# A one-core encoder-trunk step: x rows loaded for the first norm, weight chunks cut as half the features by 512 columns, and more expert rows summed on VectorE

## The chip, the cores and the metric

The kernel runs as one launch on one core of a Trainium2 chip. The metric is the device time of one execution in microseconds (us), as the median of several runs. The profile is one profiled execution of the same program.

## The reference

One layer is computed for 1024 prompt rows and 32 sample rows of 1024 features, all in float32. The sample rows are repeated four times to fill a ninth tile of 128 rows.

```python
h = rmsnorm(x, g_norm1); z = h @ w_in                 # 3096 columns: GLA q,k,v,g; low rank; FoX q,k,v; forget
o_gla, S_new = gla_recurrence(gq, gk, gv, log_a, S0)  # gated linear attention
o_fox = fox_attention(rmsnorm(fq), rmsnorm(fk), fv, cumsum(logf))
x = x + concat(o_gla_normed * silu(gg), o_fox) @ w_out
h2 = rmsnorm(x, g_norm2)
q = h2 @ w_peer_q                                     # 8 heads, two keys each of 128
s1, s2 = top16 of the products with 128 subkeys each; 16 best pairs -> idx, g = softmax(top)
a = gelu(sum_d(u_tab[idx] * h2)); x = x + sum_k(g * a * v_tab[idx])   # 8 heads x 16 experts for each row
```

Each row of x needs 128 experts, and an expert is 1024 values of u and 1024 of v. So one "slot" (one expert for each of 128 rows) is a gather of 128 rows of 8 KB, about 1.05 MB. There are 8 x 128 + 32 = 1056 slots.

## The kernel before, in words

**Front and back.** Each engine runs two interleaved programs. The *front* takes tiles through the layer in five batches: tile 0 alone, then tiles 1 and 2, 3 and 4, 5 and 6, 7 and 8. For each batch it passes the stages `mix_front` (norm and the input projection), `gla` for each tile, `attend` for each tile, `project` (w_out, the second norm) and `route` (expert choice, one head after the other). The *back* takes the 1056 slots of the tiles that are routed: while slots of tile t are worked through, the front works on later tiles. `front_plan` (line 234) gives each step of the front a cost and due times, and so fixes how many front steps stand between two slots. `drive` (line 587) emits the same interleaving on every engine. Instructions of one engine run in order, so a front instruction that waits holds up the slots behind it.

**A slot.** GpSimd issues the gather into one of 8 ring buffers (line 756), once the row that used that buffer 8 slots earlier was summed. VectorE multiplies the u half with h2 and sums (line 1694). ScalarE applies gelu for a group of two slots (line 1013). Then the v half is added, weighted, in one of two ways: on TensorE, for which ScalarE builds a diagonal matrix in two steps (lines 1010 and 1018) and TensorE adds two products of 128x512 into PSUM (line 1329), or on VectorE with one multiply-add (line 1708). `on_vector(g)` (line 278) says how many rows of group g go to VectorE; the rest goes to TensorE. The counts are 326 rows on VectorE and 730 on TensorE.

```python
stage = BESIDE[GRP * g + GRP]                  # the stage of the front at that slot
if stage == MIXING: return 2 if 0 < GRP * g < SLOTS else 1
if stage == LINEAR: return 1 if GRP * g < SLOTS else int(g % 4 == 1)
return int(g % 8 in (1, 5))                    # ROUTING
```

MIXING covers `mix_front`, `attend` and `project`; LINEAR is `gla`.

**The first norm.** x of a batch is loaded transposed (features on partitions) by ScalarE's queue near the end of the batch before. Step 0 and 1: ScalarE squares it into `mix` (line 781), after which VectorE multiplies it in place with the norm's weights (line 1390, which waits for that square). Step n+1 (n tiles in the batch): TensorE computes the 24 small columns, one tile at a time (line 1058, 8 products of 128 columns), then the sums of squares as 8 products of `mix` with a column of ones for each tile (line 1065). ScalarE takes the root (785), VectorE the reciprocal (1394), which scales z when it leaves PSUM (813).

**The projections.** Weights come by SyncE's queue in chunks of 1 MB, two buffers, each waiting for the last user. A chunk of `w_in` or `w_out` holds all 1024 features by 256 columns. For each chunk and tile TensorE does 8 products of 256 columns (line 1095, or 1254). Two chunks fill one PSUM bank of 512 columns for w_in; for w_out every chunk has its own bank and its own add by VectorE (line 1565). A float32 product is two instructions in the trace, so 8 products are x16.

## Time and profile before

| | us |
|---|---|
| three runs | 3253.04, 3254.62, 3260.53 |
| median | 3254.62 |
| the profiled execution's own time | 3254.51 |
| its span, first to last instruction | 3252.3 |

| engine | busy us | share |
|---|---|---|
| TensorE products | 2724.3 | 84% |
| VectorE | 2479.0 | 76% |
| ScalarE | 1504.6 | 46% |
| GpSimd | 1298.2 | 40% |

The 16 DMA engines move 1265 MB at a mean of 389 GB/s. Read the share of an engine as an average over stages that differ: the prologue, up to the first gather at 142.5 us, has no slots at all, and the stages after it load the engines very differently.

### The profile page before, as it was taken

The page shows a single profiled execution, that of the slowest core. Times are in us where ns is not written, and L with a number is a line of the kernel's source. Part 1 is how long each engine was busy: PE and PEld are TensorE (multiplying, and loading weights), DVE is VectorE, ACT ScalarE, POOL GpSimd, SP SyncE. Part 2 cuts the span into 40 slices and gives each one's busy share as a digit, 9 for nine tenths or more (in the row PEclk, how much of TensorE's full clock was granted, in tenths as well). Part 3 has the DMA queues.
Part 4 walks back from the last instruction along what each step waited for, and adds up shares of the span by engine and source line. Part 5 has one row for each costly group of instructions (what it writes and reads, how often), then busy time and mean ns, then how long its engine had stood idle before and what let it go on. Part 6 is the DMA issues. An engine that isn't in the chain of part 4 may idle for free. (4 is left out here: it accounts for less than half of the span.)

```text
span 3252.3 us, 34906 instructions
## 1 busy us (share of the span) xinstructions
PE 2724.3 (84%) x9716; PEld 1630.8 (50%) x9716; DVE 2479.0 (76%) x5478; ACT 1504.6 (46%) x3956; POOL 1298.2 (40%) x1062
## 2 busy tenths in 40 slices
PE   7769788887988888878988898887988898888777
PEld 6647456443753455445644464544653446444322
DVE  2487887998668868997677776998668776878864
ACT  2342463554335754454245654544236663444532
POOL 0134333444344434433443444443444434444443
PEclk9789859998999999998998899998999999999989
DMA  6399988999999999998999899999999999999998
GB/s 264 137 380 379 372 326 346 421 414 411 371 421 421 416 410 399 420 414 360 421 420 393 351 405 393 417 421 379 418 421 402 416 376 406 417 421 421 412 417 349
DMA packets 183273, 1265.12 MB, mean 389 GB/s; under 512 B 23224, under 2 KB 26696, under 8 KB 32040
## 3 DMA queue, kind: packets, MB, share of 16 engines
q0 software_dynamic: 152064, 1107.36, 83.4%
q1 hardware_dynamic: 28184, 146.17, 11.1%
q10 hardware_dynamic: 2832, 9.37, 0.8%
q8 instruction: 77, 1.26, 0.2%
q14 instruction: 116, 0.95, 0.1%
HBM read 1253.83 MB, written 9.00 MB: 388 GB/s over the span
## 5 line engine op out<-in xcount | busy, mean ns | idle before, releaser
L756 POOL DMA_INDIRECT uv_ring<-in_peer_uv,expert_index x1056 | 1293.4, 1225 | 1931.4 <-PE ps_acc L1329 1490.6
L1329 PE MATMUL ps_acc<-uv_ring,coef_diag 128*128 128x512 f32 x2920 | 1479.9, 648 | 403.4 <-ACT coef_diag L1018 383.4
L1694 DVE CUSTOM_DVE_ANT_0 uv_ring<-uv_ring,h_rows 128x1024 f32<-128x1024 f32 x1056 | 1281.2, 1219 | 402.4 <-DMA uv_ring<-in_peer_uv,expert_index 397.3
L1329 PEld LDWEIGHTS ps_acc<-uv_ring,coef_diag 128*128 128x128 f32 x2920 | 569.3, 205 | 1079.3 <-issue 544.7
L1013 ACT ACTIVATE gelu_u_dot_h<-u_dot_h 128x2 f32<-128x2 f32 x528 | 107.2, 203 | 1334.1 <-DVE u_dot_h L1694 1328.7
L1708 DVE SCALAR_TENSOR_TENSOR v_sums<-uv_ring,coefficients,v_sums 128x1024 f32<-128x1024 f32 x318 | 407.5, 1281 | 36.9 <-ACT coefficients L1020 34.7
L1095 PE MATMUL ps_scores<-weight_chunk,rows_T 128*128 128x256 f32 x1568 | 362.4, 387 | 8.3 <-DMA weight_chunk<-in_w_in_chunks 8.3
L1095 PEld LDWEIGHTS ps_scores<-weight_chunk,rows_T 128*128 128x128 f32 x1568 | 302.6, 194 | 80.9 <-issue 30.7
L1018 ACT ACTIVATE coef_diag<-coef_diag,gelu_u_dot_h 128x128 f32<-128x128 f32 x730 | 267.6, 396 | 16.3
L1286 PE MATMUL ps_turn<-rows_T,weight_chunk 128*128 128x256 f32 (+1 forms) x1280 | 267.5, 364 | 3.3 <-ACT rows_T L918 2.8
L1010 ACT ACTIVATE coef_diag<-packed_consts,expert_weight 128x128 f32<-128x128 f32 x730 | 261.3, 388 | 0.4
L1286 PEld LDWEIGHTS ps_turn<-rows_T,weight_chunk 128*128 128x128 f32 x1280 | 228.6, 196 | 55.1 <-issue 30.8
L1013 ACT ACT_TABLE_LOAD x175 | 224.5, 1283 | 14.2 <-DVE u_dot_h L1694 11.0
L1162 PE MATMUL ps_scores<-k_pairs_T,mixing_or_attention 64*128 64x512 f32 (+4 forms) x240 | 126.1, 610 | 12.7 <-ACT mixing_or_attention L878 7.9
L1543 DVE TENSOR_REDUCE neg_max<-ps_scores 128x1 f32<-128x128 f32 (+8 forms) x72 | 58.2, 810 | 83.5 <-PE ps_scores L1165 83.5
L1254 PE MATMUL ps_scores<-weight_chunk,rows_T 128*128 128x256 f32 x512 | 116.2, 384 | 0.8 <-DMA weight_chunk<-in_w_out_chunks 0.8
L1179 PEld LDWEIGHTS ps_out<-v_rows,mixing_or_attention 128*128 128x128 f32 x720 | 100.1, 210 | 28.8 <-issue 21.6
L1254 PEld LDWEIGHTS ps_scores<-weight_chunk,rows_T 128*128 128x128 f32 x512 | 98.6, 193 | 23.0 <-issue 7.4
L1179 PE MATMUL ps_out<-v_rows,mixing_or_attention 128*128 128x64 f32 x720 | 100.6, 290 | 5.2 <-ACT mixing_or_attention L888 5.1
L975 ACT ACT_TABLE_LOAD x71 | 91.1, 1283 | 1.3
L1020 ACT ACTIVATE coefficients<-gelu_u_dot_h,expert_weight 128x1 f32<-128x1 f32 x326 | 88.5, 280 | 1.0
L1694 DVE DVE_READ_ACCUMULATOR2_ANT u_dot_h<- 128x1 f32 x1056 | 86.2, 82 | 0.0
(194 smaller groups left out, 2302.0 us busy)
## 6 DMA issues: line engine op xcount, KB each, us to landing
weight_chunk<-in_w_in_chunks SPq DMA_DIRECT2D x50, 1024.0 KB
weight_chunk<-in_w_peer_q_and_subkeys SPq DMA_DIRECT2D x40, 1152.0 KB
uv_ring<-in_peer_uv,expert_index POOLq DMA_INDIRECT x1056
weight_chunk<-in_w_out_chunks SPq DMA_DIRECT2D x16, 1024.0 KB
uv_ring<-in_w_in_chunks SPq DMA_DIRECT2D x10, 1024.0 KB, 14.3
x_mid<-in_x_rows SPq DMA_DIRECT2D x9, 512.0 KB, 12.5
uv_ring<-in_w_out_chunks SPq DMA_DIRECT2D x4, 1024.0 KB, 11.9
rows_T<-in_x_T ACTq DMA_DIRECT2D x4, 1024.0 KB, 9.1
```

What stands on the lines that cost most here:

```text
L756: pool.indirect_dma_start(out=ring[:, s % RING, :], out_offset=None, in_=dram["uv"], in_offset=bass.IndirectOffsetOnAxis(ap=idx[:, t % IDX ...
L1010: act.activation(diag[:, (GRP * g + n) % RING, :], matrix[:], ACT.Copy, scale=gw[:, t % IDX, i + n:i + n + 1]).then_inc(dgw, 1)
L1013: act.activation(gel[:, g % 2, :], dots[:, g % 2, :], ACT.Gelu).then_inc(geld, 1)
L1018: act.activation(diag[:, r, :], diag[:, r, :], ACT.Copy, scale=gel[:, g % 2, n:n + 1]).then_inc(dgd, 1)
L1095: mm = pe.matmul(S[:, lo:lo + CW], xT(ts[i])[:, k, :], w[:, k * CW:(k + 1) * CW], start=(k == 0), stop=(k == KD - 1), skip_group_check=True)
L1162: pe.matmul(S[:, lo + x:lo + y], fqT[a:a + FD, pair, :], kT[a:a + FD, pair, x:y], start=True, stop=False)
L1179: mm = pe.matmul(O[:, h, :], pT[k % 2][0:blocks[n], n - 4 * q, :], v[0:blocks[n], n, h * FD:(h + 1) * FD], start=(n == 0), stop=(n == len( ...
L1254: mm = pe.matmul(S[:, 512 * (step % 3):512 * (step % 3) + CW], xT(ts[i])[:, k, :], w[:, k * CW:(k + 1) * CW], start=(k == 0), stop=(k == K ...
L1286: mm = pe.matmul(pq_ps[q % 2][:, c, 0:n * P], w[:, k * CW + c * DKEY:k * CW + (c + 1) * DKEY], turned(ts)[:, k, :, :], start=(k == 0), sto ...
L1329: mm = pe.matmul(acc[:, c, :], diag[:, r, :], ring[:, r, D + c * 512:D + (c + 1) * 512], start=first, stop=False, skip_group_check=True)
L1694: dve.tensor_tensor_reduce(out=ring[:, s % RING, 0:D], in0=ring[:, s % RING, 0:D], in1=h2[:], scale=1.0, scalar=0.0, op0=ALU.mult, op1=ALU ...
L1708: dve.scalar_tensor_tensor(out=sums[:, b, :], in0=ring[:, (GRP * g + x) % RING, D:], scalar=coef[:, g % 2, x:x + 1], in1=so_far, op0=ALU.m ...
```

## The change

- `on_vector`: in a MIXING stage beside the slots of tiles 1 to 7, groups have 1 and 2 rows on VectorE in turn where they had 1 (the slots of tile 0 keep 2). In a LINEAR stage beside tile 0 they have 0 and 1 in turn where they had 1. With the plan unchanged, 92 groups get one row more and 5 groups one less: 413 rows on VectorE, 643 on TensorE.
- The sum of squares of the first norm: x is also loaded as rows into `mix` (9 loads of 512 KB: tile 0 first on ScalarE's queue, the others on SyncE's queue ahead of the last two chunks of the batch before). ScalarE squares the rows with its accumulator, and takes the root at once in the same step. The ones products are gone, and VectorE's multiply no longer waits for a square. The reciprocal moves from step n+2 to the steps 1 to n.
- The 24 small columns of both tiles are one set of 8 products of 256 columns.
- A chunk of `w_in` or `w_out` is 512 features by 512 columns, still 1 MB: for each chunk and tile 4 products of 512 columns. Two chunks complete a bank; VectorE adds w_out's result once in two chunks, 512 columns wide.

```diff
     if stage == MIXING:
-        return 2 if 0 < GRP * g < SLOTS else 1
+        return 2 if 0 < GRP * g < SLOTS else 1 + g % 2
     if stage == LINEAR:
-        return 1 if GRP * g < SLOTS else int(g % 4 == 1)
+        return g % 2 if GRP * g < SLOTS else int(g % 4 == 1)
...
+        def rows(bi, ts):
+            sp.wait_ge(q_t, fills_before(ts[0]))
+            for i, t in enumerate(ts):
+                sp.dma_start(mix[i][:], dram["xr"][t]).then_inc(xr_in[i], 16)
...
             for c in range(IN_CH + ahead, CHUNKS):
                 chunk(bi, c)
+                if c == CHUNKS - 3 and bi + 1 < len(BATCHES):
+                    rows(bi + 1, BATCHES[bi + 1])
...
     def _(act):
+        act.dma_start(mix[0][:], dram["xr"][0]).then_inc(xr_in[0], 16)
...
-                    act.wait_ge(xT_in, 16 * (bi + 1))
-                    wait(act, q_t, fills_before(t0))
-                    act.activation(mix[i][:].rearrange("p (k t) -> p k t", k=KD), xT(t), ACT.Square).then_inc(x_sq, 1)
-                if step == n + 2:
-                    for i, t in enumerate(ts):
-                        act.wait_ge(x_ss, t0 + n)
-                        act.activation(std[:, i:i + 1], ss_ps[i], ACT.Sqrt, bias=eps[:], scale=1.0 / D).then_inc(x_std, 1)
+                    act.wait_ge(xr_in[i], 16 * (round_of(t) + 1))
+                    act.activation(mix[i][:], mix[i][:], ACT.Square, accum_out=ss[:, i:i + 1]).then_inc(x_sq, 1)
+                    act.wait_ge(x_sq, t + 1)
+                    act.activation(std[:, i:i + 1], ss[:, i:i + 1], ACT.Sqrt, bias=eps[:], scale=1.0 / D).then_inc(x_std, 1)
...
                 if step == n + 1:
                     wait(pe, o_n, t0)
-                    for i, t in enumerate(ts):
-                        pe.wait_ge(x_g, t + 1)
-                        for k in range(KD):
-                            mm = pe.matmul(zsT_ps[i], w_small[:, k, :], xT(ts[i])[:, k, :], start=(k == 0), stop=(k == KD - 1), skip_group_check=True)
-                        mm.then_inc(zs_mm, 1)
+                    pe.wait_ge(x_g, t0 + n)
+                    for k in range(KD):
+                        mm = pe.matmul(O_flat[0:LR + FH, 0:n * P], w_small[:, k, :], turned(ts)[:, k, :, :], start=(k == 0), stop=(k == KD - 1),
+                                       skip_group_check=True)
+                    mm.then_inc(zs_mm, n)
...
-                    for i, t in enumerate(ts):
-                        pe.wait_ge(x_sq, t + 1)
-                        for k in range(KD):
-                            mm = pe.matmul(ss_ps[i], mix[i][:, k * P:(k + 1) * P], ones, start=(k == 0), stop=(k == KD - 1), skip_group_check=True)
-                        mm.then_inc(x_ss, 1)
...
-                    lo = 512 * (q % 3) + CW * half
-                    for k in range(KD):
-                        mm = pe.matmul(S[:, lo:lo + CW], xT(ts[i])[:, k, :], w[:, k * CW:(k + 1) * CW],
+                    lo = WIDE * (q % 3)
+                    for k in range(HALF_K):
+                        mm = pe.matmul(S[:, lo:lo + WIDE], xT(ts[i])[:, HALF_K * half + k, :], w[:, k * WIDE:(k + 1) * WIDE],
...
-                    dve.wait_ge(x_sq, t + 1)
                     dve.tensor_tensor(xT(t), xT(t), g1[:].unsqueeze(2).to_broadcast([P, KD, P]), ALU.mult).then_inc(x_g, 1)
-                if step == n + 2:
-                    for i, t in enumerate(ts):
-                        dve.wait_ge(x_std, t + 1)
-                        dve.reciprocal(rstd[:, i:i + 1], std[:, i:i + 1]).then_inc(x_rs, 1)
+                if 0 < step <= n:
+                    i, t = step - 1, ts[step - 1]
+                    dve.wait_ge(x_std, t + 1)
+                    dve.reciprocal(rstd[:, i:i + 1], std[:, i:i + 1]).then_inc(x_rs, 1)
...
-                    half = xr[i][:, c * CW:(c + 1) * CW]
-                    bank = 512 * ((step - 1) % 3)
-                    dve.tensor_tensor(half, half, S[:, bank:bank + CW], ALU.add).then_inc(xm_r, 1)
+                    half = xr[i][:, c // 2 * WIDE:(c // 2 + 1) * WIDE]
+                    bank = WIDE * (q % 3)
+                    dve.tensor_tensor(half, half, S[:, bank:bank + WIDE], ALU.add).then_inc(xm_r, 1)
```

## Rows read from the trace of the kernel before

**Rows 1.** The page: span, busy time of two engines, DMA in all

```profile
span 3252.3 us, 34906 instructions
...
PE 2724.3 (84%) x9716; PEld 1630.8 (50%) x9716; DVE 2479.0 (76%) x5478; ACT 1504.6 (46%) x3956; POOL 1298.2 (40%) x1062
...
DMA packets 183273, 1265.12 MB, mean 389 GB/s; under 512 B 23224, under 2 KB 26696, under 8 KB 32040
```

**Rows 2.** The stretches: busy us of each engine, granted clock, DMA share, GB/s

```profile
0.00:137.00 137.00, 110.66 (x544) 93.85 (x544) 36.20 (x120) 34.93 (x74) 4.82 (x6) 0.84 0.46 171
...
230.00:250.00 20.00, 17.94 (x76) 15.16 (x77) 12.92 (x18) 6.28 (x14) 4.75 (x4) 0.59 0.56 204
...
345.00:420.00 75.00, 50.06 (x237) 27.99 (x235) 70.91 (x160) 42.33 (x93) 25.15 (x22) 0.77 0.89 340
420.00:530.00 110.00, 89.68 (x344) 66.02 (x344) 84.69 (x122) 54.16 (x129) 36.94 (x31) 0.68 0.92 355
530.00:545.00 15.00, 14.73 (x49) 9.73 (x50) 10.60 (x17) 4.92 (x12) 3.52 (x4) 0.87 0.50 183
...
805.00:830.00 25.00, 25.00 (x124) 19.26 (x123) 13.05 (x21) 6.66 (x18) 7.50 (x6) 0.89 0.66 244
830.00:960.00 130.00, 118.83 (x453) 83.17 (x451) 80.74 (x135) 39.81 (x114) 55.53 (x43) 1.00 1.01 421
...
1060.00:1175.00 115.00, 99.06 (x421) 54.91 (x422) 93.12 (x134) 86.54 (x182) 55.49 (x45) 0.97 1.01 409
...
1505.00:1530.00 25.00, 25.00 (x118) 19.30 (x117) 12.99 (x20) 6.23 (x17) 6.44 (x6) 0.83 0.60 226
...
1780.00:1900.00 120.00, 108.55 (x437) 58.91 (x437) 88.09 (x119) 80.39 (x163) 54.06 (x43) 0.90 0.92 358
...
2258.00:2275.00 17.00, 17.00 (x94) 14.14 (x92) 14.23 (x22) 6.76 (x20) 4.31 (x3) 0.90 0.63 254
...
2548.00:2700.00 152.00, 134.61 (x573) 73.06 (x573) 112.25 (x151) 92.17 (x196) 66.54 (x54) 0.94 0.97 387
```

**Rows 3.** Instructions in order of time, TensorE and GpSimd, start of tiles 3 and 4

```profile
806.42 3.87 PE L1058 MATMUL ps_out<-rows_T,w_in_small 128*24 128x128 f32 x32
...
810.22 3.86 PE L1065 MATMUL ps_out<-packed_consts,mix_rows 128*128 128x1 f32 x32
...
813.94 5.25 PE L1095 MATMUL ps_scores<-weight_chunk,rows_T 128*128 128x256 f32 x16
...
819.03 1.88 PE L1329 MATMUL ps_acc<-uv_ring,coef_diag 128*128 128x512 f32 x4
...
820.75 3.62 PE L1095 MATMUL ps_scores<-weight_chunk,rows_T 128*128 128x256 f32 x16
...
821.69 1.18 POOL L756 DMA_INDIRECT uv_ring<-in_peer_uv,expert_index  x1 [11.96 <-PE ps_acc L1329]
```

**Rows 4.** Who waited for whom over the whole span (us in total, times, longest)

```profile
POOL uv_ring L756 <- PE ps_acc L1329: 1490.6, 623, 13.1
...
DVE x_rstd L1394 <- ACT x_std L785: 26.6, 5, 7.6
...
DVE rows_T L1390 <- ACT mix_rows L781: 11.5, 4, 6.0
```

**Rows 5.** Instructions in order of time, TensorE, the prologue

```profile
13.93 3.58 PE L1065 MATMUL ps_out<-packed_consts,mix_rows 128*128 128x1 f32 x16
...
17.36 12.79 PE L1095 MATMUL ps_scores<-uv_ring,rows_T 128*128 128x256 f32 x48
...
30.72 14.08 PE L1095 MATMUL ps_scores<-uv_ring,rows_T 128*128 128x256 f32 x64
```

**Rows 6.** Groups by line and form, and one DMA issue (KB each)

```profile
L1329 PE MATMUL ps_acc<-uv_ring,coef_diag 128*128 128x512 f32 x2920 | 1479.9, 648 | 403.4 <-ACT coef_diag L1018 383.4 <-DVE v_sums L1726 14.8 <-issue 4.6
...
L1708 DVE SCALAR_TENSOR_TENSOR v_sums<-uv_ring,coefficients,v_sums 128x1024 f32<-128x1024 f32 x318 | 407.5, 1281 | 36.9 <-ACT coefficients L1020 34.7 <-issue 2.0
...
x_mid<-in_x_rows SPq DMA_DIRECT2D x9, 512.0 KB, 12.5
```

More of the change, by code:

```diff
@@ L60 @@
 OUT_CH = D // CW
+HALF_K = KD // 2
+WIDE = 2 * CW
 CHUNKS = IN_CH + OUT_CH + PH
@@ L123, in cols_before, with adds_before @@
     return OUT_CH * tiles_before(bi)
+def adds_before(bi):
+    return D // WIDE * tiles_before(bi)
 def gla_at(ts):
@@ L332, in stream @@
     iota = consts[:, 4 * P + 2:]
-    ones = tri[:, 0, P - 1:P]
     identb = sb("ident_b", [P, P], BF16)
@@ L361, in stream @@
     bT = [sb(f"b_T{i}", [P, GP, P]) for i in range(NB)]
+    ss = sb("x_sumsq", [P, NB])
     std = sb("x_std", [P, NB])
@@ L459, in stream @@
     zsT_ps = [O_flat[0:LR + FH, P * i:P * (i + 1)] for i in range(NB)]
-    ss_ps = [O_flat[:, 2 * P + i:2 * P + i + 1] for i in range(NB)]
     la_ps = [Q_flat[i][:, 0:GATES + FH] for i in range(NB)]
@@ L474, in stream @@
     xT_in = sem("x_T_loaded")
+    xr_in = [sem(f"x_rows_loaded{i}") for i in range(NB)]
     res_in = [sem(f"x_residual_loaded{i}") for i in range(NB)]
@@ L481, in stream @@
     x_sq = sem("x_squared")
-    x_ss = sem("x_sums_of_squares_done")
     x_std = sem("x_std_ready")
@@ L905, in project @@
                     t = ts[i]
-                    act.wait_ge(xm_r, cols_before(bi) + (OUT_CH - 1) * n + i + 1)
+                    act.wait_ge(xm_r, adds_before(bi) + n + i + 1)
                     act.wait_ge(q_t, mix_fill(t) + 2)
@@ L1092, in mix_front @@
                         wait(pe, z_ev, q - 2)
-                    lo = 512 * (q % 3) + CW * half
-                    for k in range(KD):
-                        mm = pe.matmul(S[:, lo:lo + CW], xT(ts[i])[:, k, :], w[:, k * CW:(k + 1) * CW],
-                                       start=(k == 0), stop=(k == KD - 1), skip_group_check=True)
+                    lo = WIDE * (q % 3)
+                    for k in range(HALF_K):
+                        mm = pe.matmul(S[:, lo:lo + WIDE], xT(ts[i])[:, HALF_K * half + k, :], w[:, k * WIDE:(k + 1) * WIDE],
+                                       start=(half == 0 and k == 0), stop=(half == 1 and k == HALF_K - 1), skip_group_check=True)
                     mm.then_inc(z_mm, 1)
@@ L1241, in project @@
                     c, i = divmod(step, n)
-                    y = cols_before(bi) + step
+                    cols, half = divmod(c, 2)
+                    q = cols * n + i
                     chunk = CHUNKS * bi + IN_CH + c
@@ L1250, in project @@
                         pe.wait_ge(ex, FH * (ts[-1] + 1))
-                    if step >= 3:
-                        pe.wait_ge(xm_r, y - 2)
-                    for k in range(KD):
-                        mm = pe.matmul(S[:, 512 * (step % 3):512 * (step % 3) + CW], xT(ts[i])[:, k, :], w[:, k * CW:(k + 1) * CW],
-                                       start=(k == 0), stop=(k == KD - 1))
+                    if half == 0 and q >= 3:
+                        pe.wait_ge(xm_r, adds_before(bi) + q - 2)
+                    lo = WIDE * (q % 3)
+                    for k in range(HALF_K):
+                        mm = pe.matmul(S[:, lo:lo + WIDE], xT(ts[i])[:, HALF_K * half + k, :], w[:, k * WIDE:(k + 1) * WIDE],
+                                       start=(half == 0 and k == 0), stop=(half == 1 and k == HALF_K - 1), skip_group_check=True)
                     mm.then_inc(y_mm, 1)
@@ L1296, in route @@
                     if m == 0:
-                        pe.wait_ge(xm_r, cols_before(bi + 1))
+                        pe.wait_ge(xm_r, adds_before(bi + 1))
                     if m >= 3:
@@ L1559, in project @@
             for step in range(out_steps(ts)):
-                if 0 < step <= OUT_CH * n:
-                    c, i = divmod(step - 1, n)
+                c, i = divmod(step - 1, n)
+                if 0 <= c < OUT_CH and c % 2 == 1:
+                    q = c // 2 * n + i
                     dve.wait_ge(y_mm, cols_before(bi) + step)
-                    half = xr[i][:, c * CW:(c + 1) * CW]
-                    bank = 512 * ((step - 1) % 3)
-                    dve.tensor_tensor(half, half, S[:, bank:bank + CW], ALU.add).then_inc(xm_r, 1)
+                    half = xr[i][:, c // 2 * WIDE:(c // 2 + 1) * WIDE]
+                    bank = WIDE * (q % 3)
+                    dve.tensor_tensor(half, half, S[:, bank:bank + WIDE], ALU.add).then_inc(xm_r, 1)
                 i, r = divmod(step - (OUT_CH * n + 3), 2)
@@ L1676, in reopen @@
             bi, i = PLACE[t]
-            dve.wait_ge(xm_r, cols_before(bi + 1))
+            dve.wait_ge(xm_r, adds_before(bi + 1))
             dve.wait_ge(p_rs, t + 1)
@@ L1771 @@
     dram["w_in_small"] = inp("w_in_small", np.concatenate([w_in[:, :, C_LR:C_LR + LR], w_in[:, :, C_FF:C_FF + FH]], axis=2).reshape(P, KD * (LR + FH)))
-    starts = [c + half * CW for c in (C_QK, C_GV, C_FK, C_FV, C_FQ, C_GG) for half in range(2)]
-    dram["w_in_chunks"] = inp("w_in_chunks", np.stack([w_in[:, :, c:c + CW].reshape(P, KD * CW) for c in starts]))
-    dram["w_out"] = inp("w_out_chunks", x["w_out"][0].reshape(KD, P, OUT_CH, CW).transpose(2, 1, 0, 3).reshape(OUT_CH, P, KD * CW))
+    starts = [(c, half) for c in (C_QK, C_GV, C_FK, C_FV, C_FQ, C_GG) for half in range(2)]
+    dram["w_in_chunks"] = inp("w_in_chunks", np.stack([w_in[:, HALF_K * h:HALF_K * (h + 1), c:c + WIDE].reshape(P, HALF_K * WIDE) for c, h in starts]))
+    dram["w_out"] = inp("w_out_chunks", x["w_out"][0].reshape(2, HALF_K, P, D // WIDE, WIDE).transpose(3, 0, 2, 1, 4).reshape(OUT_CH, P, HALF_K * WIDE))
     w_q = x["w_peer_q"][0].reshape(KD, P, PH, CW).transpose(2, 1, 0, 3).reshape(PH, P, KD * CW)
```

2 lines of the change are left out of this document (1 added, 1 removed).

## The prediction

> **What bounds the kernel now.** I began with the page [rows 1]: TensorE is busy for 84% of the span and VectorE for 76%, so neither share decides. Then I cut the span into stretches by stage [rows 2]. In the input projection of tiles 3 and 4 (830 to 960 us) the DMA share is 1.01 at 421 GB/s, the most that any stretch shows. At that rate the 1265 MB would take 3005 us. The span is 3252.3 us, so 247 us are DMA idleness, and that alone is what a change to the engines can win. The reader is to see in rows 2 where it lies. I count a stretch's length times (1.01 less its share): the prologue to 137 us gives 75 us; the starts of the four later batches (230 to 250, 805 to 830, 1505 to 1530, 2258 to 2275) give 9.0 + 8.8 + 10.3 + 6.5 = 34.6 us; the linear attention of tiles 1 and 2 (345 to 420) 9.0; their attention and output (420 to 530) 9.9; the attention of tiles 5 and 6 (1780 to 1900) 10.8; that of tiles 7 and 8 (2548 to 2700) 6.1; the start of routing of tiles 1 and 2 (530 to 545) 7.7. The attention of tiles 3 and 4 (1060 to 1175) has none. The rest lies in short dips and the tail.
>
> Third, the waits: GpSimd waits 1490.6 us for TensorE's sums [rows 4]. Most of that costs nothing, because gathers are queued behind a full DMA. It costs where the wait outlasts the queue. Rows 3 show such a place. At 806.42 TensorE starts the small columns (3.87 us), then the ones products (3.86), then a unit of projection (5.25), and only then the next expert row; GpSimd sat 11.96 us before its gather at 821.69.
>
> **The sum of squares.** The ones products go: 3.86 us at the start of tiles 3 and 4 [rows 3]. The small columns of two tiles become 16 instructions of 256 columns; 16 such instructions of the projection start and end within 3.62 us, against 3.87: 0.3 us. The first unit of projection took 5.25 us where the next took 3.62 [rows 3], in a stretch whose granted clock is 0.89, while the next stretch has 1.00 [rows 2]. So TensorE was at 1.2 GHz for part of it, right behind products with one column of output. With them gone I let that unit run at 3.62, which is 1.6 us. Together 5.8 us of 8.8 idle ones, two thirds. The same pattern stands at the other starts (clocks 0.59, 0.83, 0.90), so I take two thirds of 34.6: **23 us**. Bounds: the ones products alone, 4 x 3.9 = 15 us, and all 34.6. At the start of tiles 1 and 2 the rows of tile 0 are all summed on VectorE, so there VectorE's own waits count: 26.6 us for the root in 5 places and 11.5 us for the squares in 4 [rows 4]. Both end: the multiply waits for nothing but x^T, and the root comes from ScalarE without TensorE. What is late next is ScalarE: square and root of two tiles, one behind the other, for which VectorE waits one step later. It costs nothing beside the multiplies.
>
> **The prologue.** TensorE's chain decides it. The ones products take 3.5 us (13.93 to the next start at 17.36). But the first 48 instructions of projection took 12.79 us, where 64 took 14.08 later [rows 5], or 0.22 us each; 48 would be 10.6. If the slow ones take 0.44, ten of them ran at 1.2 GHz, until about 21.8 us. If the clock rises at the same moment, the removed 3.5 us were slow time and bring half, 1.75 us; if it rises earlier too, 3.5. VectorE's multiply starts up to 1 us earlier, against 512 KB more of loads at that time (0.52 MB at 421 GB/s, 1.2 us). I take **2 us**, bounds 0.5 and 4.5.
>
> **The loads of x rows.** One such load is 512 KB [rows 6]. Eight of them lie in routing stages: 8 x 0.524 = 4.2 MB, at 421 GB/s **10 us lost**, for the DMA is full there. Bounds: 4 us if they fall into dips, 10 if not. On SyncE's queue they stand between chunk 22 and 23 of a batch. Their wait (all transposes of the batch done) was met many heads earlier, and the two chunks behind come 2.5 us later, while a whole head of routing stands before each is used: nothing. On ScalarE's queue at the start the one load delays the constants by 1.2 us, which TensorE first needs for the gates, in the pause ahead of 30.72 us [rows 5].
>
> **Rows moved to VectorE.** 92 groups get one row more on VectorE, 5 one less: net 87. A row on TensorE costs 4 instructions of 1479.9 / 2920 = 0.507 us [rows 6], 2.0 us; on VectorE 1.28. So TensorE loses 176 us of work and VectorE gains 111. None of it is a gain where the DMA is full. In the input projections (36 rows) VectorE has 80.7 busy of 130 us and 43 gathers there; about 11 rows more add 14 us: free. In the attention of tiles 3 and 4 it has 93.1 of 115, and 11 rows more make 107; in 1780 to 1900 88 become 102 of 120; in 2548 to 2700 112 become 130 of 152 [rows 2]. It fits, narrowly in the first. There TensorE (99 of 115, 108.6 of 120, 134.6 of 152) is relieved, and GpSimd waits for it at every group now, for it only at every second one then. Of the 16.9 us of idleness in the last two I take **8 us** back; bounds 17 won and, as nothing shows what VectorE's late releases cost, 20 lost. Beside tile 0, in 345 to 420, VectorE is busy for 70.9 of 75 us and is what ends last: 5 rows less are 6.4 us of it, against 10 us more on a TensorE that is busy for 50. Of the 9.0 us idle I take **3 us**; bounds 0 and 6.4.
>
> **Chunks of half the features.** The same bytes, the same product columns; half as many weight loads, which run beside products. 16 instructions of 256 columns take 3.62 us, 0.88 ns for a column, and 4 of 512 columns 1.88, 0.92 ns [rows 3], so doubling the width saves nothing to speak of: 0, bounds 0 and 3 us won. The bank is shared by two chunks as before. The adds of w_out become half as many and twice as wide; the last of a tile is a little longer, under 0.5 us for each batch: nothing, and if the cover by slots is gone, 2 us.
>
> **The sum.** 23 + 2 - 10 + 8 + 3 = 26 us won, and I add 2 of the 7.7 us at the start of routing, where a gather also waits for TensorE's row behind its other waits: 28. The sum is made against the profiled execution, whose own time is 3254.51 and which equals the median of 3254.62 within 0.1. So **3226 us**. A measurement of this kernel can tell about 0.2%, 6.5 us, from no change.
>
> **Rivals.** (a) *VectorE becomes the bound in attention.* Of the 92 rows 56 lie there, 72 us of VectorE. It must also wait in order for scores of each head, and while it waits it can't release rows. Without the 8 us, 18 us are won elsewhere; when more than 18 + 2 of the 72 us show up, the kernel is slower. For it: 107 of 115 us. Against: the stretch 830 to 960 has room, and 345 to 420, where VectorE is full at 70.9 of 75, lost only 9 us. With half of the 72 exposed: 3254.5 - 20 + 36 = 3270 us. Chance 0.10. (b) *TensorE's clock takes the gain.* In 420 to 530 the granted clock is 0.68 and the DMA share only 0.92, with all rows of tile 0 on VectorE; in 1060 to 1175 it is 0.97 and the share 1.01 [rows 2]. With fewer rows TensorE has more gaps, may fall to 1.2 GHz more often, and then delays attention itself. If the three attention stages lost 9% as 420 to 530 does, that would be (115 + 120 + 152) x 0.09 = 35 us in place of the 17 they lose now: 3226 + 8 + 18 = 3252 us, no change that can be told. Chance 0.10. The Trainium skill (TensorE: Matmul & The Clock Gate, "What's actually happening") says that the throttled state is the default and that activity releases it. By that rule a lighter TensorE is a slower one; rows 2 agree for gaps but can't show where the limit lies. (c) *More comes back.* If all of the starts (34.6), the attention dips (17) and 6 in the linear stage are recovered, and prologue 4: 3254.5 - 62 + 10 = 3203 us. Chance 0.20. (d) *The norm doesn't leave the path:* the row loads come late and ScalarE waits for them at a batch's start. The issue stands two heads ahead, so 0.02; it would give back the 23 us: 3249.
>
> **How the numbers follow.** My forecast has 0.58. The range 3197 to 3256 takes in (c), (b) and (d) and leaves out (a) and the far end of (c). Faster by over 0.2% (below 3248): 0.58 + 0.20 and a little of (b): 0.80. Within: most of (b) and (d), 0.10. Slower: (a), 0.10.
>
> **What would show it.** No group of one-column products; the first projection unit of a later batch within 3.7 us; GpSimd's longest wait at the batch starts at 6 us and not 12 or 13; DMA share of those stretches from about 0.6 up to 0.85; 1270 MB in all; VectorE near 2590 us, TensorE near 2530; the first gather about 2 us earlier. I am wrong if the DMA share in 1060 to 1175 falls below 0.97 with VectorE full, or if the starts keep their dips.

## The result, and the profile after

The changed kernel is **slower by 0.4%**. Its median is 3271.10 us (3268.69 to 3277.24, 4 runs), against 3253.83 us (4 runs) of the kernel before on the same chip: a ratio of 1.0041, 95% interval 1.0024 to 1.0059. That is above the range of 3197 to 3256, and the change moved the time up where the forecast of 3226 had it fall. The profiled execution has an own time of 3268.69, against 3254.51.

The page of the kernel after, its span, busy times and DMA in all, answers to [rows 1]:

```profile
span 3266.7 us, 31552 instructions
...
PE 2648.0 (81%) x8008; PEld 1358.6 (42%) x8008; DVE 2579.3 (79%) x5547; ACT 1477.9 (45%) x3879; POOL 1308.9 (40%) x1062
...
DMA packets 184559, 1269.64 MB, mean 389 GB/s; under 512 B 23369, under 2 KB 26841, under 8 KB 33337
```

VectorE (2590 forecast, 2579.3 measured) and the bytes (1270 MB, 1269.64) are as foreseen. TensorE isn't: 2530 was forecast and 2648.0 stands there, for 1708 instructions fewer. The mean granted clock of the span fell with it: 0.883 after, 0.922 before.

The starts of the batches came out near the forecast. The timeline of the kernel after, TensorE and GpSimd at the start of tiles 3 and 4, answers to [rows 3] (start us, us, engine, line; in brackets the idle time before and what ended it). L1067 is the group of small columns, L1100 a projection, L1336 an expert row:

```profile
800.19 5.90 PE L1067 MATMUL ps_out<-rows_T,w_in_small 128*24 128x256 f32 x16 [0.90 <-DVE rows_T L1396]
806.02 3.70 PE L1100 MATMUL ps_scores<-weight_chunk,rows_T 128*128 128x512 f32 x8
809.56 1.88 PE L1336 MATMUL ps_acc<-uv_ring,coef_diag 128*128 128x512 f32 x4
811.28 7.03 PE L1100 MATMUL ps_scores<-weight_chunk,rows_T 128*128 128x512 f32 x16
...
799.57 1.29 POOL L768 DMA_INDIRECT uv_ring<-in_peer_uv,expert_index  x1 [3.98 <-PE ps_acc L1336]
...
812.22 1.38 POOL L768 DMA_INDIRECT uv_ring<-in_peer_uv,expert_index  x1 [3.32 <-PE ps_acc L1336]
```

No one-column group stands between the small columns and the first unit of projection, that unit takes 3.70 us instead of 5.25 (also at tiles 5 and 6, and 7 and 8), and GpSimd waits 3.98 and 3.32 where it waited 11.96. One size is off: the small columns take 5.90 here and not the 3.6 that was forecast. At the other starts they take 5.73, 6.51 and, as forecast, 3.61 (tiles 7 and 8). The slow part of TensorE's time now falls on them. So small columns, ones products and first unit together fell by 3.4 us here (12.98 to 9.60), where 5.8 was forecast.

The loss lies elsewhere. The stretches of the kernel after, one row each for the start of tiles 3 and 4, for the linear stage and the attention of tiles 1 and 2 beside tile 0, and for the three attention stages of tiles 3 to 8. The columns are stretch, length, busy us (count) of PE, PEld, DVE, ACT, POOL, then granted clock, DMA share and GB/s. Each stage but the first of these rows is cut at the gather with the same number in every kernel, so lengths can be subtracted:

```profile
802.00:826.00 24.00, 24.00 (x61) 10.39 (x60) 20.02 (x28) 6.97 (x23) 10.49 (x10) 0.94 1.00 407
...
300.49:389.58 89.09, 70.40 (x233) 34.51 (x232) 65.40 (x141) 40.87 (x90) 26.71 (x22) 0.85 0.93 363
389.58:488.82 99.24, 82.31 (x309) 51.69 (x308) 83.39 (x134) 53.00 (x129) 35.93 (x30) 0.62 0.86 316
1024.25:1192.88 168.63, 132.84 (x471) 69.68 (x469) 140.05 (x198) 95.33 (x212) 76.16 (x61) 0.82 0.95 386
1731.28:1952.70 221.42, 177.64 (x625) 94.52 (x624) 177.98 (x250) 118.40 (x254) 99.62 (x77) 0.80 0.93 373
2484.38:2735.26 250.88, 204.16 (x750) 108.85 (x748) 204.88 (x278) 129.85 (x280) 110.78 (x86) 0.80 0.96 383
```

The kernel before, the same three attention stages:

```profile
1032.66:1191.67 159.01, 135.59 (x558) 76.13 (x556) 125.72 (x189) 100.61 (x228) 73.31 (x60) 0.98 1.01 412
1733.32:1948.57 215.25, 192.02 (x741) 106.88 (x739) 161.05 (x240) 126.47 (x276) 91.05 (x76) 0.90 0.96 382
2479.87:2721.39 241.52, 215.40 (x867) 117.27 (x866) 179.98 (x257) 137.24 (x300) 104.88 (x86) 0.94 0.99 398
```

These stages grew from 615.8 to 640.9 us, by **25.1**, while the forecast had them 8 shorter. VectorE isn't full in any of them (140 of 169, 178 of 221, 205 of 251). What stands out is the clock: 0.98, 0.90 and 0.94 fell to 0.82, 0.80 and 0.80.

The instructions that write the rows' sum on TensorE, of 128x512, from 1024 to 1192 us; first the kernel after, then the kernel before:

```profile
1024.00:1192.00 168.00, 50.12 (x78) 17.54 (x77) 0.00 (x0) 0.82 0.95 386
```

```profile
1024.00:1192.00 168.00, 72.17 (x145) 25.66 (x144) 0.00 (x0) 0.98 1.01 413
```

78 instructions in 50.12 us are 0.64 us each; 145 in 72.17 are 0.50. So 46% fewer of them relieve TensorE by only 31%. How that reaches the DMA is seen in the timeline of the kernel after, TensorE and GpSimd in that stage, and in its stretches of 8 us. L1167 is the product of scores:

```profile
1064.52 2.07 PE L1167 MATMUL ps_scores<-k_pairs_T,mixing_or_attention 64*128 64x512 f32 x2
...
1067.89 3.48 PE L1336 MATMUL ps_acc<-uv_ring,coef_diag 128*128 128x512 f32 x4
...
1072.13 1.12 PE L1167 MATMUL ps_scores<-k_pairs_T,mixing_or_attention 64*128 64x512 f32 x2
...
1071.64 1.91 POOL L768 DMA_INDIRECT uv_ring<-in_peer_uv,expert_index  x1 [5.93 <-PE ps_acc L1336]
```

```profile
1048.00:1056.00 8.00, 2.03 (x3) 0.99 (x4) 6.93 (x10) 3.21 (x8) 2.23 (x2) 0.50 1.01 418
1056.00:1064.00 8.00, 6.13 (x25) 2.45 (x23) 7.40 (x11) 5.45 (x13) 4.30 (x4) 0.91 1.02 423
1064.00:1072.00 8.00, 8.00 (x25) 4.14 (x24) 6.96 (x11) 7.70 (x15) 1.41 (x3) 0.57 0.97 405
1072.00:1080.00 8.00, 8.00 (x40) 4.51 (x39) 7.07 (x10) 7.47 (x14) 4.96 (x5) 1.00 0.75 285
```

TensorE has little to do from 1048 to 1056 (2.03 us of 8; it waits 7.53 us for a diagonal until 1053.97) and the clock there is 0.50. From 1064 to 1072 it is 0.57 again, behind a wait of 1.87 us that ended at 1062.84. Now the stage's own work arrives and runs for the most part at 1.2 GHz: the product of scores takes 2.07 us instead of 1.12, and the row behind it 3.48, where [rows 3] has 1.88. GpSimd waits 5.93 us for that row, and the DMA share of the next 8 us is 0.75.

Cut at the same gathers, the two profiled executions account for the whole difference (us; "input" is the four later batches' norm and projection, "linear" and "attention" those of tiles 3 to 8 with the output). The 10 us forecast for the loads of x rows are split by where the loads stand in the kernel after: two of the eight are issued at 151.3 us, in the routing of tile 0, and six in the three later routing stages.

```
stage                       before   after   change   forecast
to the first gather          142.5   137.6     -4.9       -2
routing of tile 0             55.4    55.0     -0.4     +2.5
input, 4 batches             568.2   544.6    -23.6      -23
linear + att. of tiles 1, 2  179.8   188.3     +8.5       -3
routing, 3 stages            855.2   862.5     +7.3     +7.5, -2
linear, 3 stages             304.5   306.3     +1.8        0
attention, 3 stages          615.8   640.9    +25.1       -8
last routing and end         530.9   531.4     +0.5        0
sum                                           +14.3      -28
```

### The profile page after: what moved, and what is told of

It reads as the page before. It is cut to its first block and busy times, and to the rows that moved or that the text cites. A ratio compares the mean times of both kernels' runs of the same rounds, so it can differ in the third digit from the quotient of the medians.

```text
span 3266.7 us, 31552 instructions
## 1 busy us (share of the span) xinstructions
PE 2648.0 (81%) x8008; PEld 1358.6 (42%) x8008; DVE 2579.3 (79%) x5547; ACT 1477.9 (45%) x3879; POOL 1308.9 (40%) x1062
## 2 busy tenths in 40 slices
DMA packets 184559, 1269.64 MB, mean 389 GB/s; under 512 B 23369, under 2 KB 26841, under 8 KB 33337
## 5 line engine op out<-in xcount | busy, mean ns | idle before, releaser
L1336 PE MATMUL ps_acc<-uv_ring,coef_diag 128*128 128x512 f32 x2572 | 1374.5, 681 | 429.8 <-ACT coef_diag L1028 410.4
L1336 PEld LDWEIGHTS ps_acc<-uv_ring,coef_diag 128*128 128x128 f32 x2572 | 529.8, 216 | 1096.1 <-ACT coef_diag L1028 546.8
L1715 DVE SCALAR_TENSOR_TENSOR v_sums<-uv_ring,coefficients,v_sums 128x1024 f32<-128x1024 f32 x405 | 519.4, 1283 | 31.9 <-ACT coefficients L1030 28.5
L1100 PE MATMUL ps_scores<-weight_chunk,rows_T 128*128 128x512 f32 x784 | 356.3, 606 | 14.8 <-DMA weight_chunk<-in_w_in_chunks 14.7
L1100 PEld LDWEIGHTS ps_scores<-weight_chunk,rows_T 128*128 128x128 f32 x784 | 151.0, 196 | 216.1 <-issue 185.1
L1028 ACT ACTIVATE coef_diag<-coef_diag,gelu_u_dot_h 128x128 f32<-128x128 f32 x643 | 233.2, 398 | 13.3
L1020 ACT ACTIVATE coef_diag<-packed_consts,expert_weight 128x128 f32<-128x128 f32 x643 | 228.0, 390 | 0.4
L1167 PE MATMUL ps_scores<-k_pairs_T,mixing_or_attention 64*128 64x512 f32 (+4 forms) x240 | 142.3, 682 | 40.6 <-ACT mixing_or_attention L888 31.2
L1184 PEld LDWEIGHTS ps_out<-v_rows,mixing_or_attention 128*128 128x128 f32 x720 | 105.8, 223 | 36.3 <-issue 19.0
L1261 PE MATMUL ps_scores<-weight_chunk,rows_T 128*128 128x512 f32 x256 | 116.7, 610 | 5.0 <-DMA weight_chunk<-in_w_out_chunks 5.0
L1184 PE MATMUL ps_out<-v_rows,mixing_or_attention 128*128 128x64 f32 x720 | 108.4, 304 | 14.3 <-ACT mixing_or_attention L898 14.2
L1030 ACT ACTIVATE coefficients<-gelu_u_dot_h,expert_weight 128x1 f32<-128x1 f32 x413 | 106.4, 286 | 4.3 <-ACT gelu_u_dot_h L1023 0.3
L898 ACT ACTIVATE mixing_or_attention<-ps_turn 128x512 f32<-128x512 f32 (+3 forms) x112 | 53.1, 501 | 83.6 <-PE ps_turn L1177 79.0
```

What stands on the lines that cost most here:

```text
L1020: act.activation(diag[:, (GRP * g + n) % RING, :], matrix[:], ACT.Copy, scale=gw[:, t % IDX, i + n:i + n + 1]).then_inc(dgw, 1)
L1028: act.activation(diag[:, r, :], diag[:, r, :], ACT.Copy, scale=gel[:, g % 2, n:n + 1]).then_inc(dgd, 1)
L1100: mm = pe.matmul(S[:, lo:lo + WIDE], xT(ts[i])[:, HALF_K * half + k, :], w[:, k * WIDE:(k + 1) * WIDE], start=(half == 0 and k == 0), stop ...
L1167: pe.matmul(S[:, lo + x:lo + y], fqT[a:a + FD, pair, :], kT[a:a + FD, pair, x:y], start=True, stop=False)
L1184: mm = pe.matmul(O[:, h, :], pT[k % 2][0:blocks[n], n - 4 * q, :], v[0:blocks[n], n, h * FD:(h + 1) * FD], start=(n == 0), stop=(n == len( ...
L1261: mm = pe.matmul(S[:, lo:lo + WIDE], xT(ts[i])[:, HALF_K * half + k, :], w[:, k * WIDE:(k + 1) * WIDE], start=(half == 0 and k == 0), stop ...
```

## The experiments

The theory behind the first three runs was rival (b): the moved rows make TensorE emptier, its clock falls, and everything it still does is late. The rival to that was (a): VectorE's additional adds are late, and the clock is a bystander.

How far one profile can be trusted is seen where two versions have the same code in a stage. The three attention stages together come to 625.6 and 622.2 us in two versions that are alike there, and to 640.9, 641.6 and 642.9 in the three that have the moved rows there and sum them in full. So a difference under 4 us in this sum can't be told from none. The input stage of tiles 1 and 2 took 111.6 and 108.3 us in two versions with the same code in it.

**Rows moved beside the input projection only.** The changed kernel, with attention, output and linear stages as before:

```diff
-MIXING, LINEAR, ROUTING = range(3)
+MIXING, LINEAR, ROUTING, INPUT = range(4)      # INPUT: the steps of mix_front
+    if stage == INPUT:
+        return 2 if 0 < GRP * g < SLOTS else 1 + g % 2
     if stage == MIXING:
-        return 2 if 0 < GRP * g < SLOTS else 1 + g % 2
+        return 2 if 0 < GRP * g < SLOTS else 1
     if stage == LINEAR:
-        return g % 2 if GRP * g < SLOTS else int(g % 4 == 1)
+        return 1 if GRP * g < SLOTS else int(g % 4 == 1)
```

> The changed kernel, with 3 of 4 rows on VectorE only beside the input projection (and 2 of 4 beside attention and output, all of them beside the linear stage of tiles 1 and 2, as before). If the moved rows are what costs time in attention, whether by VectorE's load or by TensorE's clock, the three attention stages give back their 25 us and the linear stage of tiles 1 and 2 its 5.5 us, and the input stages keep their 24 us: about 3241 us, faster than before. If the new chunk shapes or the row loads slow attention, it stays near 3271.

(In the linear stage of tiles 1 and 2 it is one row of two that VectorE sums, as the diff shows, and not all of them.)

Measured: 3242.46 us, ratio 0.9951 (0.9935 to 0.9968), faster than both kernels. The stretches of the three attention stages:

```profile
1019.34:1183.39 164.05, 142.40 (x524) 72.44 (x523) 125.41 (x186) 100.68 (x227) 75.66 (x60) 0.93 1.00 401
1719.44:1933.94 214.50, 188.38 (x700) 97.35 (x699) 160.55 (x237) 126.33 (x276) 95.01 (x76) 0.92 0.96 384
2462.60:2709.68 247.08, 218.77 (x833) 114.25 (x832) 182.79 (x259) 137.95 (x303) 103.42 (x86) 0.92 0.97 392
```

They sum to 625.6 us, 15.3 less than after, and the linear stage with the attention of tiles 1 and 2 comes to 181.6 (188.3 after). So the loss is in the rows of these stages. Whether by clock or by VectorE this run doesn't say.

**Idle products in place of the moved rows.** The changed kernel; wherever in attention or output a row was moved off TensorE, it gets two products of 128x512 with zero weights, added into the sum. They add nothing to the result:

```diff
+                    if extra(g):               # attention or output of tiles 3 to 8, and VECTOR[g] == 2
+                        for c in range(2):
+                            pe.matmul(acc[:, c, :], zeros[:], g2[:, c * 512:(c + 1) * 512], start=False, stop=False, ...)
```

> The changed kernel, with two products of 128x512 more on TensorE (zero weights, so nothing is added to the sums) for each of the 56 rows moved in attention and output. TensorE has its old load there, VectorE keeps the new one. Clock theory: the granted clock in the three attention stages rises from 0.80-0.82 to 0.9 or more and they lose their extra 25 us: about 3246. VectorE theory: the stages stay at 169, 221 and 251 us, 3271 or a little more.

Measured: 3255.51 us, ratio 1.0007 (0.9992 to 1.0021), against 1.0041 (1.0024 to 1.0059) of the kernel after. The same three stretches:

```profile
1028.92:1194.68 165.76, 146.69 (x525) 75.57 (x524) 139.86 (x199) 95.12 (x212) 78.89 (x61) 0.90 0.97 392
1733.71:1949.93 216.22, 188.03 (x695) 97.90 (x694) 177.80 (x250) 118.02 (x254) 98.23 (x76) 0.91 0.96 384
2483.36:2726.24 242.88, 216.93 (x833) 113.06 (x832) 205.35 (x279) 129.29 (x280) 111.48 (x86) 0.92 0.99 398
```

VectorE does as much as after (523.0 us in the three, 522.9 after), TensorE does useless work besides, and the stages are 624.9 us, **16.0 less** than after. The clock is back at 0.90 to 0.92. No account by VectorE's load can give this. The clock theory had expected all 25 us back and 3246 in all, so it holds for some two thirds of the loss.

**Moved rows' adds cut short.** The changed kernel; VectorE adds only 64 of the 1024 columns of each row that was moved in these stages, so that part of those rows is missing from the sum:

```diff
-                    dve.scalar_tensor_tensor(out=sums[:, b, :], in0=ring[:, ..., D:], ..., in1=so_far, ...)
+                    w = 64 if extra(g) and n == 1 else D
+                    dve.scalar_tensor_tensor(out=sums[:, b, 0:w], in0=ring[:, ..., D:D + w], ..., in1=so_far[:, 0:w], ...)
```

> The changed kernel, with VectorE's multiply-add of each of the 56 moved rows in attention and output cut to 64 of 1024 columns: those rows are left out of 960 columns of the sum. TensorE has its new light load, VectorE about its old one. Clock theory: granted clock stays at 0.80-0.82 and so does the time, 3271. VectorE theory: the attention stages give back their 25 us although the clock stays low, about 3246.

Measured: 3267.59 us, ratio 1.0032 (1.0013 to 1.0051). The same stretches:

```profile
1026.75:1192.10 165.35, 135.30 (x471) 70.40 (x469) 126.06 (x195) 95.26 (x212) 72.33 (x61) 0.81 0.96 385
1730.91:1949.98 219.07, 173.97 (x624) 92.22 (x623) 161.97 (x250) 118.37 (x254) 94.12 (x76) 0.82 0.92 371
2480.07:2731.82 251.75, 204.76 (x751) 110.23 (x750) 185.33 (x278) 129.48 (x280) 104.38 (x87) 0.80 0.96 383
```

VectorE's busy time is back at that of the kernel before (126, 162, 185 against 126, 161, 180), and the stages are only 4.7 us shorter than after (636.2). The clock stays at 0.80 to 0.82. So the VectorE theory, which expected 25 us back, is out as the main cause. The two runs part the price of the moved rows: 16.0 us by TensorE's clock, which is shown, and 4.7 by VectorE, which is likely and not shown: it is little more than the spread of the sum, and the interval of the ratio (1.0013 to 1.0051) overlaps that of the kernel after. Their sum, 20.7, is near the 19.2 between the kernel after and the next version, which leaves the rows where they were.

**All rows as before, norm and chunks as after.**

```diff
     if stage == MIXING:
-        return 2 if 0 < GRP * g < SLOTS else 1 + g % 2
+        return 2 if 0 < GRP * g < SLOTS else 1
     if stage == LINEAR:
-        return g % 2 if GRP * g < SLOTS else int(g % 4 == 1)
+        return 1 if GRP * g < SLOTS else int(g % 4 == 1)
```

> The changed kernel with the rows shared out as before: only the norm by loaded rows and the new chunks. The dips at the four batch starts are won by the norm, so most of the 24 us of the input stages stays, the 10 us of loads are paid, attention is as before: about 3243. If the rows beside the input projection were what closed the dips, the input stages are back at their old times and it is near 3260.

Measured: 3247.09 us, ratio 0.9975 (0.9957 to 0.9992). The attention stages take 621.7 us, the input stages 549.6, that is 18.6 of the 23.6 us won there, before any row is moved. The first version of this section, with rows moved beside the input projection, is 4.6 us faster by medians that were measured together (3242.46), 1.7 of it in the input stages; the two intervals overlap a little, so this gain is likely and not shown. The next three runs each take one part of the change alone.

**The new `on_vector` alone**, in the kernel before:

> The kernel before with only the new shares of rows (413 on VectorE). Clock theory: the three attention stages lose about 20 us at a granted clock near 0.8, the linear stage of tiles 1 and 2 loses 4, the input stages win 2 to 5: about 18 us slower than before, ratio 1.0055. If the rows only hurt together with the new chunks, it is within 6 us of before.

Measured: 3279.24 us, ratio 1.0072 (1.0048 to 1.0097). Attention 641.6 (+25.8, at granted clocks of 0.79, 0.80 and 0.80), linear and attention of tiles 1 and 2 192.0 (+12.2), input 557.7 (-10.5). The moved rows alone lose more than the whole change does. In the input stages they win 10.5 us by themselves and the norm alone 19.8 (below), but together 23.6. Perhaps both shorten the same waits; the runs don't show it.

**The chunks alone**, in the kernel before:

> The kernel before with only the new chunks. By the prediction nothing moves: within 3 us of before. But the attention and output of tiles 3 and 4 stayed at 164 to 166 us in all four kernels with the norm and the chunks, against 159 before; if the chunks do that, this one shows about 165 there at a granted clock of 0.93 and is 5 us slower in all.

Measured: 3259.29 us, ratio 0.9996 (0.9981 to 1.0012), and no row of the table moved by over 2.1 us. The attention of tiles 3 and 4 took 161.4, not 165, so the chunks are not what makes it longer in the versions that have them together with the norm.

**The norm alone**, in the kernel before:

> The kernel before with only the norm by loaded rows (and the small columns of both tiles at once). The starts of the batches give 18 us, the prologue 3 to 5, the loads cost 8 to 10: 12 to 14 us faster than before, ratio 0.996. If part of the win at the starts came from the chunks, it is under 8 us.

Measured: 3245.78 us, ratio 0.9963 (0.9942 to 0.9983). Input 548.4 (-19.8), routing 863.0 (+7.8), attention 620.1 (+4.3). It is 13.5 us faster than the kernel before, as expected.

**Without the row loads of tiles 3 to 8.** The changed kernel, but six of the nine loads of x rows are left out. ScalarE squares and sums what lies in `mix`, so those tiles are scaled by other roots and gather other experts:

```diff
-                if c == CHUNKS - 3 and bi + 1 < len(BATCHES):
+                if c == CHUNKS - 3 and bi == 0:
                     rows(bi + 1, BATCHES[bi + 1])
```

> The changed kernel without the loads of x rows for tiles 3 to 8; ScalarE squares what lies in the buffers, so those tiles are scaled by wrong roots and pick other experts. 6 loads of 0.524 MB are gone: at 421 GB/s 7.5 us. If they are paid in full, about 3263 us; if they were hidden, 3271.

Measured: 3263.05 us, ratio 1.0016 (1.0001 to 1.0031), 0.25% or 8 us below the kernel after; the two intervals overlap a little. Six loads of 0.524 MB at 421 GB/s are 7.5 us. The three routing stages take 855.5 us, as before the change (855.2; after 862.5), although the experts differ. So the six loads cost about what their bytes take.

The last two runs ask how far the clock theory carries.

**One row of two on TensorE beside tile 0 too.** The best version so far; in the attention of tiles 1 and 2, where VectorE summed both rows of a group, it sums one:

```diff
     if stage == MIXING:
-        return 2 if 0 < GRP * g < SLOTS else 1
+        return 1
```

> The version of e1_rows_by_stage, but in attention and output of tiles 1 and 2, beside the expert rows of tile 0, VectorE sums one row of two and TensorE the other, where VectorE summed both. Before, in that stretch (420 to 530 us) TensorE was busy for little of the time, its granted clock was 0.68 and the DMA share 0.92, some 10 us idle. Theory (a TensorE with more product rows keeps its clock, and the gathers keep the DMA full): the clock of that stage rises from about 0.7 to 0.85 or more, the stage becomes 3 to 7 us shorter than in e1_rows_by_stage, and the whole time falls by as much. Rival (rows on TensorE are late there because its own work is serial, as in the linear stage beside tile 0, where two rows more on it cost 4 us): the clock rises but GpSimd waits for TensorE's sums instead of VectorE's, and the stage becomes 3 to 8 us longer.

Measured: 3241.45 us, ratio 0.9950 (0.9931 to 0.9968). The attention of tiles 1 and 2, first in this run, then in the version that it starts from:

```profile
391.81:484.94 93.13, 76.15 (x348) 42.62 (x347) 72.78 (x127) 58.35 (x146) 34.31 (x30) 0.93 0.88 333
```

```profile
388.06:484.63 96.57, 78.70 (x299) 50.48 (x298) 84.67 (x137) 52.95 (x129) 35.71 (x31) 0.61 0.87 324
```

The clock rose from 0.61 to 0.93. (TensorE had not been idle for most of this stage, as the expectation says: it was busy for 81% of it.) TensorE has 49 instructions more there and is busy for 2.6 us less. The stage is 3.4 us shorter, the least that the theory asked for. The whole time shows no gain that can be told from 3242.46, and the DMA share hardly rose (0.87 to 0.88), so something else than the clock bounds this stage. Nor does the run part the clock from VectorE, which is relieved of 12 us here. From the 84th to the 102nd gather GpSimd waited 39.3 us for VectorE's sums and none for TensorE's in the version that it starts from; in this run it waits 34.2 us for TensorE's and none for VectorE's. The wait changed engines and hardly got shorter.

**Idle products on top of the best version**, behind every group of attention and output of tiles 3 to 8, where TensorE still has one row of two:

```diff
-    return ... BESIDE[GRP * g + GRP] == MIXING and VECTOR[g] == 2
+    return ... BESIDE[GRP * g + GRP] == MIXING
```

> The version of e1_rows_by_stage with two products with zero weights (128x512, added into the sum, so they add nothing) behind each group of expert rows while attention and output of tiles 3 to 8 run. There e1_rows_by_stage has granted clocks of 0.93, 0.92 and 0.92 in the three stages and takes 625.6 us for them, 10 us more than the kernel before. Theory (clock follows how full TensorE is, and time follows the clock): the clocks rise to 0.96 or more, and the three stages come to 612 to 620 us, 5 to 12 us less. Rival (0.92 is enough, the rest of those 10 us has another cause, and TensorE is now nearly full, so that idle products only delay its scores): the three stages take 625 to 640 us, whatever the clock.

Measured: 3331.28 us, ratio 1.0221 (1.0203 to 1.0239):

```profile
1017.42:1203.36 185.94, 177.14 (x629) 89.25 (x628) 124.53 (x186) 101.57 (x227) 73.84 (x60) 0.98 0.92 360
1744.79:1986.94 242.15, 231.57 (x836) 118.36 (x835) 160.60 (x237) 126.36 (x276) 93.75 (x76) 0.99 0.91 349
2518.87:2794.66 275.79, 268.11 (x989) 137.47 (x988) 181.75 (x259) 139.17 (x303) 111.76 (x86) 0.99 0.91 357
```

The clock did what the theory said (0.98 to 0.99); the time didn't. The stages take 703.9 us, 78 more, outside what either side expected. TensorE is busy for 95 to 97% of them: at full clock it has too much to do. So "more clock is less time" holds only while the engine has gaps. Of the amounts tried, one row of two on TensorE is the best for these stages; with less, or with idle products on top, time is lost.

## Why the prediction was wrong

**The step that failed is "Rows moved to VectorE"**: "Of the 16.9 us of idleness in the last two I take 8 us back", with 20 lost as the other bound. The three attention stages lost 25.1 us instead. The step counted the work taken from TensorE as 4 x 0.507 us a row, which supposes that the rest runs as fast as before, and asked of VectorE only whether it fits. It did fit: that part of the argument held, and the adds cost some 4.7 us by the run with short adds. But the rows that were taken away were also what kept TensorE's clock up. The forecast of 2530 us for TensorE missed by 118 us. The rows' instructions fell from 1479.9 us [rows 6] to 1374.5, by 105 where 176 was forecast: that is 71 of the 118. Attention's own products, whose number didn't change, grew by 39: the products of scores from 126.1 to 142.3 us, the transposes behind them (L1177) from 61.9 to 71.2, the products with v (L1184) from 100.6 to 108.4, and two smaller groups by 6.

The sign that the prediction had named for being wrong came by half. In 1060 to 1175 the DMA share fell below 0.97, to 0.92, but VectorE was busy for 95.9 of 115 us there and not full; the clock was 0.79, where [rows 2] has 0.97:

```profile
1060.00:1175.00 115.00, 93.29 (x360) 52.61 (x358) 95.93 (x131) 77.16 (x160) 52.64 (x41) 0.79 0.92 370
```

The mechanism had been named, as rival (b), at 0.10. It was priced by the 9% that 420 to 530 loses [rows 2]: three stages would go from 17 lost to 35, so 18 more. By the runs the clock takes 16.0, near those 18, and VectorE perhaps 4.7. Rival (a) had named 3270 us, and 3271.10 was measured, but by luck: its mechanism accounts for those 4.7 and not for the 36 that it had exposed. Some 4 to 5 us of the 25.1 remain in any case: the four versions with the new norm and the old rows take 620.1 to 625.6 us in these stages, where the two with the old norm take 615.8 and 617.6. The runs don't explain this; with the rows moved the norm made no such difference (640.9 and 641.6).

What should have shifted the chances stood in [rows 2]: 420 to 530, where all rows of tile 0 are on VectorE, has 0.68, and 1060 to 1175, the same kind of work with one row of two on TensorE, has 0.97. That pair is the change's own experiment, already made in the kernel before; the prediction quoted it for rival (b) and gave it 0.10. The Trainium skill (TensorE: Matmul & The Clock Gate, "What's actually happening") says that throttling is the default and activity releases it. By that rule a lighter TensorE was a slower one, and the runs agree: with less work the clock was 0.79 to 0.82, with useless work in its place 0.90 to 0.92.

**The linear stage beside tile 0**: 3 us won was forecast, within 0 and 6.4. Linear and attention of tiles 1 and 2 lost 8.5; 6.7 of it goes away when the old rule is put back (181.6). VectorE was relieved nearly as foreseen (65.4 us busy after, 70.4 before). The clock was no lower than before: 0.85 after, 0.84 before. What failed is the reading of "a TensorE that is busy for 50" of 75 us as room. The row that comes back stands right behind one that is already late. First a group with both rows on TensorE in the kernel after, then a group with one in the version with all rows as before:

```profile
338.61 6.39 PE L1336 MATMUL ps_acc<-uv_ring,coef_diag 128*128 128x512 f32 x8 [3.41 <-ACT coef_diag L1028]
```

```profile
344.74 3.78 PE L1336 MATMUL ps_acc<-uv_ring,coef_diag 128*128 128x512 f32 x4 [3.11 <-ACT coef_diag L1028]
```

TensorE idles until the group's diagonal is there. One row then takes 3.78 us, where it takes 1.88 in [rows 3], so it runs at 1.2 GHz; two rows take 6.39, that is 2.6 more. GpSimd, which waits for these sums to free its buffers, waits for them 30.6 us between the 60th and the 72nd gather, where it waits 24.7 with the old rows, and that stretch takes 46.9 us and not 42.4. From the 72nd to the 84th, where attention begins, it is 39.2 and not 36.6; the cause of that part stays open.

**The sum of squares**: the mechanism was right, and the size nearly. 23 won was forecast for it; the norm alone won 18.6 to 19.8. The 23.6 of the input stages holds some 4 to 5 more, which come with the rows that were moved and had been put at nothing, so that the two totals agree so well is luck. The DMA share at the four starts is 0.86, 1.00, 0.99 and 0.87, where 0.85 was forecast. The first projection unit takes 3.70 at three of the four starts, and at tiles 1 and 2 three units take 10.57. GpSimd's longest waits around the four starts are 4.8 to 7.2, where 6 was forecast. That the clock at a start is low because of the one-column products is not shown: without them the small columns were slow.

**The prologue**: 2 was forecast and 4.9 stands in the table, but one profile can't carry that. The first group of products there, in the kernel after and then in the version with the new `on_vector` alone, whose prologue is that of the kernel before ([rows 5]: 13.93 3.58 and 17.36 12.79):

```profile
9.61 3.53 PE L1067 MATMUL ps_out<-rows_T,w_in_small 128*24 128x128 f32 x16 [9.61 <-DVE rows_T L1396]
13.07 10.57 PE L1100 MATMUL ps_scores<-uv_ring,rows_T 128*128 128x512 f32 x24
```

```profile
12.92 1.95 PE L1065 MATMUL ps_out<-packed_consts,mix_rows 128*128 128x1 f32 x16
14.72 10.61 PE L1095 MATMUL ps_scores<-uv_ring,rows_T 128*128 128x256 f32 x48
```

The same program had its ones products at 1.2 GHz in 3.58 us once and mostly at 2.4 GHz in 1.95 the other time, and its projection in 12.79 and 10.61. The first gather came at 142.5, 142.0 and 137.3 us in the three profiles with the old norm, and at 136.5 to 139.9 in the nine with the new one, 138.0 on average. The means differ by 2.6 us, near the forecast of 2, but the spread within either set is larger (3.4 and 5.2), so the gain is not shown.

**The loads of x rows**: 10 lost was forecast, with 4 as the other end, and 2 won at the start of routing. The three routing stages lost 7.3, and 7.8 with the norm alone. Leaving out six loads brought back 7.0 there and 8 in all, for 7.5 computed. The two loads beside the routing of tile 0 show no cost (55.0 us after, 55.4 before), and the 2 us at the start of routing didn't come. **The chunks**: 0, as forecast.

Put together: 3226 plus 33 for the attention stages and 11.5 beside tile 0, 1 for all the rest, less 3 for the prologue, is some 3268; the profiled execution has 3268.69. Two readings within the one step carry most of the miss: rows taken from TensorE were priced as if the rest kept its speed, and rows given back to it as if they ran in its gaps.

## What to carry to other kernels

Before work is moved off a TensorE that isn't full, look at the granted clock of that stage beside stages of the same kind with less work: where the emptier one has the lower clock, price what remains at that lower clock, and only then count the relief. Put rows where the engine's gaps are filled and not where its own work is serial; moving them beside the input projection, where TensorE is nearly full, cost nothing and probably won a little, and moving them beside attention lost 19 us. Idle products show whether the clock is the cause, but they are a probe, not a remedy: the version that wins (3242 us, ratio 0.9951) has none.

## What the runs showed of the hardware

- A row (4 instructions of 128x512) took 1.88 us in a stretch with a clock of 0.94 and 3.48 in a stretch with 0.57. Over the stage, a mean of 0.64 us for an instruction at a clock of 0.82 and 0.50 at 0.98.
- In three attention stages the clock was 0.79 to 0.82 in the versions with the moved rows (TensorE busy for 79 to 83%), 0.90 to 0.98 with the old rows or idle products in their place (85 to 90%), and 0.98 to 0.99 with idle products on top (95 to 97%). Within the middle group the order doesn't hold: the kernel before has 0.98 at 85% and 0.90 at 89%. The busy time is itself longer at a low clock, so these are no rule. Beside tile 0 more work even lowered the busy time (78.7 to 76.2 us) by raising the clock from 0.61 to 0.93.
- The clock's rise in the prologue is not a property of the program: two executions of the same instructions, in two kernels with the same prologue, had their first group of projection in 12.79 and in 10.61 us.
